# Expert gate and up, retention input and first modulation weights laid out by the host, 4 KB to a partition

## What is computed

```python
c_act = jax.nn.silu(c)
for i in range(2):
    mod = c_act @ ada_w + ada_b
    sh1, sc1, g1, sh2, sc2, g2 = jnp.split(mod, 6, axis=-1)
    h = modulate(rmsnorm(x, n1), sh1, sc1)
    m = retention_mixer(h, *mix_p, row, col) if i == 0 else gqa_mixer(h, *mix_p, row, col)
    x = x + g1[:, None, :] * m
    h = modulate(rmsnorm(x, n2), sh2, sc2)
    f = swiglu(h, *ffn_p) if i == 0 else moe_swiglu(h, *ffn_p)
    x = x + g2[:, None, :] * f
return modulate(rmsnorm(x, final_norm_g), fsh, fsc)

# retention: proj = h @ w_in            w_in (1024, 6144)
# moe: top 2 of 8 experts;  swiglu = (silu(h @ w_gate) * (h @ w_up)) @ w_down
#      w_gate, w_up (8, 1024, 3584), w_down (8, 3584, 1024)
```

## Time and profile before

| | us |
|---|---|
| Median of three runs | 1553.6 |
| The three runs | 1553.60, 1554.18, 1545.27 |
| The profiled execution, its own time | 1550.78 |
| Its span, first to last instruction | 1548.6 |
| TensorE busy | 1493.6 (96%) |
| VectorE busy | 1340.8 (87%) |
| ScalarE busy | 992.5 (64%) |
| GpSimd busy | 206.8 (13%) |
| Moved by DMA | 508.71 MB, mean 328 GB/s |

### The profile page before, as it was taken

The page is one execution under the profiler, slowest core; times in us unless marked ns, Lnnn a source line. Parts: engine busy times, 40 slices in busy tenths (PEclk is TensorE's granted clock), DMA queues, the critical chain, the costliest instruction groups (busy, mean ns, idle before and its releaser), DMA issues.

```text
span 1548.6 us, 20483 instructions
## 1 busy us (share of the span) xinstructions
PE 1493.6 (96%) x6796; PEld 1221.8 (79%) x6796; DVE 1340.8 (87%) x1083; ACT 992.5 (64%) x826; POOL 206.8 (13%) x188
## 2 busy tenths in 40 slices
PE   6999998999999999999999999999999999999996
PEld 6777676788877787778888888888888888887885
DVE  6899878888889689998998988988888988988898
ACT  4554344444447566677777777777777777777674
POOL 0499800000020011001001001001001001000320
PEclk9999999999999989999999999999999999999999
DMA  9989826899875379999999999999999999999993
GB/s 338 390 302 350 294 80 233 283 314 310 295 267 177 108 285 356 389 343 384 387 362 381 385 371 372 384 368 370 384 369 366 393 368 371 386 368 333 391 394 139
DMA packets 238897, 508.71 MB, mean 328 GB/s; under 512 B 15494, under 2 KB 38150, under 8 KB 238728
## 3 DMA queue, kind: packets, MB, share of 16 engines
q1 hardware_dynamic: 233824, 491.52, 87.2%
q0 software_dynamic: 4448, 14.55, 2.6%
q10 hardware_dynamic: 584, 2.11, 0.3%
HBM read 502.12 MB, written 7.87 MB: 329 GB/s over the span
## 4 chain that ended last, share of the span: by engine, by line
PE 72%; DVE 9%; POOL 7%; DMA 5%; ACT 3%; issue 3%; SPq 1%; ACTq 0%; DVEq 0%; POOLq 0%
PE bank L2051 22%; PE bank L2053 22%; PE bank L2052 22%; DVE lo L1794 3%; DMA stage<-in_l_moe_w_up 2%; PE bank L2475 1%; POOL proj L655 1%; POOL proj L654 1%; POOL ropet L651 1%; POOL ropet L650 1%; POOL ropet L652 1%; POOL proj L653 1%; DMA stage<-in_l_moe_w_gate 1%; PE bank L2157 1%; DMA stage<-in_l_ret_w_in 1%
## 5 line engine op out<-in xcount | busy, mean ns | idle before, releaser
L1794 DVE TENSOR_TENSOR lo<-stage,hi 128x2048 fp32r<-128x2048 f32 x168 | 388.4, 2319 | 41.9 <-ACT hi L1118 41.2
L1118 ACT CAST hi<-stage 128x2048 fp32r<-128x2048 f32 x168 | 321.9, 1918 | 106.0 <-DMA stage<-in_l_moe_w_up 91.1
L2052 PE MATMUL bank<-lo,hg_hi 128*128 128x512 f32 x892 | 348.2, 390 | 0.0
L772 ACT CAST hi<-stage 128x2048 fp32r<-128x2048 f32 x68 | 130.3, 1918 | 106.8 <-PE bank L2053 78.4
L2052 PEld LDWEIGHTS bank<-lo,hg_hi 128*128 128x128 f32 x892 | 168.1, 188 | 33.4
L1260 DVE TENSOR_TENSOR lo<-stage,hi 128x2048 fp32r<-128x2048 f32 x68 | 157.2, 2315 | 24.0 <-ACT hi L772 18.1
L1794 DVE TENSOR_TENSOR lo<-stage,hi_h 128x2048 fp32r<-128x2048 f32 x56 | 128.3, 2292 | 55.9 <-ACT hi_h L1118 55.9
L2051 PE MATMUL bank<-hi,hg_hi 128*128 128x512 f32 x448 | 174.5, 390 | 1.0 <-DVE lo L1794 1.0
L2052 PE MATMUL bank<-lo,eaT_hi 128*128 128x512 f32 x448 | 174.4, 389 | 0.0
L2053 PE MATMUL bank<-hi,hg_lo 128*128 128x512 f32 x448 | 174.3, 389 | 0.0
L2051 PE MATMUL bank<-hi,hT_hi 128*128 128x512 f32 x400 | 162.7, 407 | 2.3 <-DVE hT_lo L1323 2.1
(11 more groups left out here) (378 smaller groups left out, 2801.7 us busy)
## 6 DMA issues: line engine op xcount, KB each, us to landing
stage<-in_l_moe_w_gate SPq DMA_DIRECT2D x224, 512.0 KB, 5.1
stage<-in_l_moe_w_up SPq DMA_DIRECT2D x224, 512.0 KB, 5.6
stage<-in_l_moe_w_down SPq DMA_DIRECT2D x224, 512.0 KB, 5.4
ada_w<-in_l_ada_w SPq DMA_DIRECT2D x40, 1024.0 KB, 5.7
stage<-in_l_ret_w_in SPq DMA_DIRECT2D x48, 512.0 KB, 8.7
stage<-in_l_ffn_w_gate SPq DMA_DIRECT2D x22, 512.0 KB, 7.5
stage<-in_l_ffn_w_up SPq DMA_DIRECT2D x22, 512.0 KB, 8.7
stage<-in_l_ffn_w_down SPq DMA_DIRECT2D x22, 512.0 KB, 8.5
```

What stands on the lines that cost most here:

```text
L772: nc.scalar.copy(hi_of(b), stage[:, b % RING, :]).then_inc(hi_done, 1)
L1118: nc.scalar.copy(hi_e(b), stage[:, b % RING, :]).then_inc(hi_done, 1)
L1794: nc.vector.tensor_tensor(lo[:, b % RING, :], stage[:, b % RING, :], hi_e(b).bitcast(F32), ALU.subtract).then_inc(lo_done, 1)
L2052: mm(dst_ap, a_hi, w_lo, start=False, stop=False)
```

## The change

The host lays four tensors out anew before the launch, and the loads follow. A unit of `l0_ret_w_in`, `l1_moe_w_gate` and `l1_moe_w_up` becomes 128 rows of 2048 contiguous floats, one to a partition, so that each of its two DMAs is the first or second 4 KB of every 8 KB row (`load_laid`). A new input, `ada_pre`, holds the columns of shift and scale of the first modulation matrix, so that a piece of `pre_w` is one contiguous 4 KB a partition. The order of the loads, their sizes, their waits and semaphores, and what is in each buffer afterwards are as before. The other tensors keep their form. The host's work lies outside the time.

```diff
             l1_moe_w_router, l1_moe_b_router, l1_moe_w_gate, l1_moe_w_up, l1_moe_w_down,
-            final_ada_w, final_ada_b, final_norm_g, consts, dist, columns, out):
+            final_ada_w, final_ada_b, final_norm_g, consts, dist, columns, ada_pre, out):
     ctx = ExitStack()
...
-        w_in_v, w_out_v = rows(l0_ret_w_in), rows(l0_ret_w_out)
+        w_out_v = rows(l0_ret_w_out)
         fg_v, fu_v, fd_v = rows(l0_ffn_w_gate), rows(l0_ffn_w_up), rows(l0_ffn_w_down)
         qkv_v, ao_v = rows(l1_attn_w_qkv), rows(l1_attn_w_out)
-        mg_v = l1_moe_w_gate.rearrange("e (k p) n -> e p k n", p=P)
-        mu_v = l1_moe_w_up.rearrange("e (k p) n -> e p k n", p=P)
         md_v = l1_moe_w_down.rearrange("e (k p) n -> e p k n", p=P)
...
+            def load_laid(b, src, more=0):
+                sp.wait_ge(w_used, b + more + 1)
+                for part in (slice(0, UW // 2), slice(UW // 2, UW)):
+                    sp.dma_start(stage[:, b % RING, part], src[:, part]).then_inc(w_load[b % RING], 16)
             def load_ada(c, half, w, bias, col, more=0):
...
-                src = rows(l0_ada_w)[:, k, 0:2 * D].rearrange("p (s n) -> p s n", s=2)
-                sp.dma_start(pre_w[half][:, k], src[:, :, half * HALF:(half + 1) * HALF]).then_inc(pre_load[half * KT + k], 16)
+                src = ada_pre[half * KT + k].rearrange("p (s n) -> p s n", s=2)
+                sp.dma_start(pre_w[half][:, k], src).then_inc(pre_load[half * KT + k], 16)
...
                 cc, kg = in_unit(u)
-                load(U_RET + u, w_in_v[:, 4 * kg:4 * kg + 4, cc * CB:(cc + 1) * CB])
+                load_laid(U_RET + u, l0_ret_w_in[2 * cc + kg])
...
                 load_pre(0, k)
-            first = stage[:, 0, :].rearrange("p (k n) -> p k n", k=4)
-            sp.dma_start(first[:, 0:2, :], w_in_v[:, 0:2, 0:CB]).then_inc(w_first, 16)
+            sp.dma_start(stage[:, 0, 0:UW // 2], l0_ret_w_in[0, :, 0:UW // 2]).then_inc(w_first, 16)
             sp.sem_inc(w_load[0], 16)
-            sp.dma_start(first[:, 2:4, :], w_in_v[:, 2:4, 0:CB]).then_inc(w_load[0], 16)
+            sp.dma_start(stage[:, 0, UW // 2:UW], l0_ret_w_in[0, :, UW // 2:UW]).then_inc(w_load[0], 16)
             load_in(1)
...
                 load(U_AOUT + k, ao_v[:, 4 * kg:4 * kg + 4, n * CB:(n + 1) * CB])
-            def load_gate_up(e, b, col, more):
-                for m, wv in ((0, mg_v), (2, mu_v)):
+            def load_gate_up(e, b, j, more):
+                for m, wv in ((0, l1_moe_w_gate), (2, l1_moe_w_up)):
                     for g in range(2):
-                        load(b + m + g, wv[e, :, 4 * g:4 * g + 4, col] if isinstance(e, int) else
-                             wv[bass.ds(e, 1), :, 4 * g:4 * g + 4, col].rearrange("a p k n -> p (a k) n"), more)
+                        at_row = j * (2 * P) + g * P
+                        load_laid(b + m + g, wv[e, bass.ds(at_row, P), :] if isinstance(e, int) else
+                                  wv[bass.ds(e, 1), bass.ds(at_row, P), :].rearrange("a p n -> p (a n)"), more)
...
                     jm = j * 6 - 6
-                    load_gate_up(e, U_MOE + 4, bass.ds(j * ECH, ECH), more + jm)
+                    load_gate_up(e, U_MOE + 4, j, more + jm)
                     load_down(e, U_MOE + 8, j * 4 - 4, more + jm)
...
-            load_gate_up(0, U_MOE, slice(0, ECH), 0)
+            load_gate_up(0, U_MOE, 0, 0)
             for half in range(2):
...
                 before = sp.value_load(meta[0:1, bass.ds(w - 1, 1)], min_val=0, max_val=E - 1)
-                load_gate_up(e, U_MOE - 2, slice(0, ECH), w * UNITS_ITEM)
+                load_gate_up(e, U_MOE - 2, 0, w * UNITS_ITEM)
                 load_down(before, U_MOE + 2, 4 * (N_EC - 1), w * UNITS_ITEM)
...
     given["columns"] = np.ascontiguousarray(np.concatenate([v.reshape(-1, P).T for v in first], axis=1))
+    pre = given["l0_ada_w"][:, 0:2 * D].reshape(KT, P, 2, 2, HALF)
+    given["ada_pre"] = np.ascontiguousarray(pre.transpose(3, 0, 1, 2, 4)).reshape(2 * KT, P, 2 * HALF)
+    w_in = given["l0_ret_w_in"].reshape(2, 4, P, N_IN, CB)
+    given["l0_ret_w_in"] = np.ascontiguousarray(w_in.transpose(3, 0, 2, 1, 4)).reshape(2 * N_IN, P, UW)
+    for name in ("l1_moe_w_gate", "l1_moe_w_up"):
+        w = given[name].reshape(E, 2, 4, P, N_EC, ECH)
+        given[name] = np.ascontiguousarray(w.transpose(0, 4, 1, 3, 2, 5)).reshape(E, N_EC * 2 * P, UW)
     arrays, args = {}, []
...
```

## The result

| | before | after |
|---|---|---|
| Median, 20 runs each | 1549.9 us | 1554.4 us |
| Lowest and highest | 1543.4, 1554.2 | 1551.8, 1561.1 |
| Ratio after to before, 95% interval | | 1.0039 (1.0027 to 1.0051) |
| Profiled execution, its time | 1550.8 | 1556.6 |
| Its span | 1548.6 | 1554.5 |

The kernel is slower by 0.4%: the two medians differ by 4.5 us, the ratio stands for 6 us. The forecast was 5 to 6 us less, 1547.5 us. The time lies in the stated range and within 1% of before, but it moved the other way. That it lies in the range is no merit of the sum: its upper end, 1556, was set from no gain at the highest of the three runs known then (median 1553.6), and the median of twenty runs before is 1549.9.

The account below looks back on a forecast made before the run. TensorE was taken to set the pace in the middle items, with transfers hidden. Terms 0.5 + 2.0 + 0.5 + 1.0 + 1.0 = 5.0 us, and 1.1 more, off 1553.6 gave 1547.5 us, range 1539 to 1556.

Parts of the forecast that it names:

- What bounds the kernel: Middle items of expert work: TensorE sets the pace at 2.84 us a unit, SP waits for buffers, transfers are hidden.
- The transfer term: Gate and up units: 4 KB packets save 0.12 us a unit, 2.71 to 2.59, bounds 0 and twice that.
- Issue: SP's issue of a gate DMA falls from 383 ns to near 345 ns, which gains nothing.
- The start: 0 to 60 us: earlier first piece 0.1 and no wait before `lo` 0.4, together 0.5 us less.
- The first item: 565 to 670 us: VectorE bounds; faster transfer in four chunks gives 2.0 us less, bounds 0 and 3.3.
- The items in the middle: Short cast delays at the seams between items: 0.5 us less, bounds 0 and 0.7.
- The rival with the other sign: New layout slower to read, deciding above 2.97 us a unit; 1570 us at 3.05; chance of over 1% slower 0.06.
- The last item: 1386 to 1505 us: 1.0 us less from the long wait, bounds 0 and 4.0, and 1.0 from the `lo` waits.
- A sign of the forecast: Whole kernel: packets fewer by a third to a half at the same bytes.
- The 1.1 us that I took off the median: Whole kernel: besides the sum, 1.1 us less because faster transfers may shorten late transfers in the slower runs.

Follow-up runs that it names:

- e4_2kb_packets: The changed kernel's layout, but gate and up loaded in packets of 2 KB, 2 KB of every 4 KB; ratio to the kernel before 1.0191.
- e7_pitch_10kb: The changed kernel with 2 KB of padding behind each 8 KB row of gate and up; ratio to the kernel before 0.9963.
- e5_rows_early: The changed kernel with the split of the next item's rows moved ahead of the second gate unit's cast and split; ratio to the kernel before 1.0000.
- e2_experts_only: The kernel before with only gate and up in the new form, start loads as before; ratio to the kernel before 1.0069.
- e3: The changed kernel, but each half of a gate or up unit is one piece of 512 KB in HBM; ratio to the kernel before 0.9976.
- e1_start_only: The kernel before with only retention input and first modulation in the new form, gate and up as before; ratio to the kernel before 0.9996.
- e11_pitch_18kb: The changed kernel with gate and up rows side by side plus 2 KB padding, 4 KB of every 18 KB; ratio to the kernel before 0.9981.

## Why the prediction was wrong

*What bounds the kernel.* Right: middle items run at TensorE's pace, SP waits for buffers. The six items between the first and the last seam are full, but for one late landing at most, with every layout whose median landing is 5 us or less.

*The transfer term.* Right in sign and near in size where the DMA engines are saturated. Casts that waited in the first item, start us first:

```profile
603.38 1.92 ACT L1122 CAST hi<-stage 128x2048 fp32r<-128x2048 f32 x1 [0.17 <-DMA stage<-in_l_moe_w_down]
605.92 1.92 ACT L1122 CAST hi_m<-stage 128x2048 fp32r<-128x2048 f32 x1 [0.63 <-DMA stage<-in_l_moe_w_down]
...
608.76 1.91 ACT L1122 CAST hi_h<-stage 128x2048 fp32r<-128x2048 f32 x1 [0.43 <-DMA stage<-in_l_moe_w_gate]
611.31 1.92 ACT L1122 CAST hi_r<-stage 128x2048 fp32r<-128x2048 f32 x1 [0.64 <-DMA stage<-in_l_moe_w_gate]
```

Gate units now come 608.76 to 611.31, 2.55 us apart instead of 2.71, down 2.54. The saving, 0.16 us, is above my 0.12 and inside its bound of twice that. Two of the experiments say what it hangs on. Two gate units of e4_2kb_packets, 2 KB of every 4 KB, and two of e7_pitch_10kb, 4 KB of every 10 KB, in the same stretch:

```profile
603.07 1.91 ACT L1127 CAST hi_h<-stage 128x2048 fp32r<-128x2048 f32 x1 [0.31 <-DMA stage<-in_l_moe_w_gate]
605.78 1.92 ACT L1127 CAST hi_r<-stage 128x2048 fp32r<-128x2048 f32 x1 [0.80 <-DMA stage<-in_l_moe_w_gate]
```

```profile
603.03 1.91 ACT L1122 CAST hi_h<-stage 128x2048 fp32r<-128x2048 f32 x1 [0.15 <-DMA stage<-in_l_moe_w_gate]
605.59 1.92 ACT L1122 CAST hi_r<-stage 128x2048 fp32r<-128x2048 f32 x1 [0.65 <-DMA stage<-in_l_moe_w_gate]
```

They are 2.71 and 2.56 us apart. So in a full queue packets of 2 KB take 2.71 us a unit at pitches of 4 and 14 KB, packets of 4 KB take 2.55 us at 8 and 10 KB: the rate follows the packet, not the pitch. The Trainium skill's fixed cost of a packet ("DMA: Bandwidth & Descriptors", "Why small descriptors are slow (HBM only)"), by which I had estimated 0.06 us, gives too little here.

*Issue.* Right. SP's gate issue went from 383 to 333 ns in the median and changed nothing:

```profile
L503 SPq DMA_DIRECT2D stage<-in_l_moe_w_gate x224: 327/333/1070, 489.5 to 1505.1; - x112
```

*The start.* The steps were right. The wait of 0.42 us before `lo` is gone, and VectorE's steps keep their 1.3 us:

```profile
9.37 0.75 DVE L1350 TENSOR_SCALAR hs<-pre_w,cact 128x1024 f32<-128x1024 f32 x1 [9.25 <-DMA pre_w<-in_ada_pre]
...
12.67 9.19 DVE L1352 SCALAR_TENSOR_TENSOR hs<-pre_w,cact,hs 128x1024 f32<-128x1024 f32 x7
...
32.72 2.29 DVE L1264 TENSOR_TENSOR lo<-stage,hi 128x2048 fp32r<-128x2048 f32 x1
34.93 7.88 DVE L1352 SCALAR_TENSOR_TENSOR hs<-pre_w,cact,hs 128x1024 f32<-128x1024 f32 x6
```

The last six start at 34.93 instead of 36.24, 1.3 us earlier, where I had 0.5: the first piece landed 0.9 us earlier (9.37 instead of 10.24), not 0.1. But it came back at once. TensorE, which had stood idle for these steps, starts its next work earlier and is on the lower of its two clock levels: the mean granted clock of the stretch 45 to 60 is 0.75 after. It was 0.80 before:

```profile
45.00:60.00 15.00, 15.00 (x61) 12.74 (x61) 10.30 (x15) 8.03 (x8) 1.09 (x2) 0.80 1.04 393
```

Rotation on GpSimd starts at 60.86 after and 60.84 before. The experiment with the start alone (0.9996) agrees that the net is nothing I can measure. I had put the term down as kept because the work behind it was full; I had not asked at which clock that work starts. When the lower clock falls differs from one execution to the next, so these two settle no more than themselves: with the same start layout, the execution of e5_rows_early has 1.00 in this stretch and its rotation starts at 56.71, and with the old start e2_experts_only has 0.89 and 58.67.

*The first item.* Direction right, size too large. The waits for `eact` fell from 4.0 to 2.1 us, which looks like the 2.0 us of the term, but only one of them fell for the change. These end the second of the four chunks, before and after:

```profile
631.45 0.66 PE L2475 MATMUL bank<-cst,eact 128*128 128x128 f32 x4 [1.44 <-DVE eact L1849]
```

```profile
633.20 0.66 PE L2479 MATMUL bank<-cst,eact 128*128 128x128 f32 x4 [0.73 <-DVE eact L1853]
```

This chunk took 18.53 us and takes 17.82, 0.7 us less. The next two took 18.67 and 18.65 us and take 18.65 and 18.63: in them ScalarE reaches a gate cast late because it waits for TensorE in front of it (2.92 us for a sum of modulation, L2026), not for a transfer. With the layouts of e2, e3, e4 and e7 these two chunks take 18.63 to 18.67 us as well, so they do not depend on the transfer. The wait of 0.89 us at 578.08 is gone, but there TensorE was at the lower clock for longer (0.97 in the stretch 565 to 670, 0.99 before) and came about 3 us later itself. e5_rows_early, with the same layouts, has 1.00 in that stretch and that wait (0.79 us), so the 3 us belong to this execution and are no part of the explanation. The term, put at 2.0 us, is worth about 0.7.

*The items in the middle: the step that failed.* I wrote that with a transfer of 2.59 us for 2.84 us of TensorE's work "in the new form these units would only wait longer for TensorE". That set a rate against a rate. The seam hangs on a latency, from SP's issue to the landing of the first gate unit, and I took it as a thing that could only shorten with the packets. It rose from 5.1 to 6.45 us at the seam shown, against a slack of about 0.2 us (VectorE done at 806.56, TensorE needs it at 806.75). Seven waits of 0.9 to 1.3 us, 7.6 us in all, outweigh the gains; from the first to the last seam the kernel takes 6.6 us more, where I had put 0.5 us less. I had bounded this term by 0 and a gain of 0.7 us, without a loss. That is the error in the sum. A row that shows how little slack there is was at hand: the wait of 2.33 us stands at a seam. I called it a chance event, which it is, but it also says that a landing a few us late is not absorbed there.

*The rival with the other sign* named the mechanism, 4 KB of every 8 KB in a regular pattern, but priced it as a rate. By that price nothing is lost until a unit takes 2.97 us, and units took 2.55. The loss begins well below that price, since latency is lost first. The evidence that I set against it, attention output weights with 2 KB of every 4 KB landing in 4.5 us, was read where the DMA engines are not full (share 0.68 from 468.7 to 487.0 us, where these units are loaded). In the experts' stage the same pattern (e4_2kb_packets) costs 1.9%. The Trainium skill's entry on row pitches of large powers of two ("DMA: Bandwidth & Descriptors", "Latency and other measured facts") starts at 512 KiB; the runs show a loss from pitches of 4, 8 and 16 KB, and its remedy, padding, works here with 2 KB. It tells the loss as a rate, while here the rate in a full queue is kept and the landing is late.

*The last item.* From its seam on it takes 2.3 us less, near the 2.0 us of my two terms, but not for their reasons, so this is luck. The long wait of 2.33 us is not repeated, and one of 1.02 us takes its place. It is absent with the old layout of gate and up too (e1_start_only, 0.2 us of seam waits in all), so it belonged to that one execution. The waits for `lo` grew from 1.0 to 1.6 us instead of vanishing.

*A sign of the forecast.* "Packets fewer by a third to a half" does not follow from its own count: 65,536 of 238,897 packets are 27%, and 27% went. The 1.1 us that I took off the median besides the sum, for late transfers in the slower runs, is shown by no run.

**What stays open.** No run here shows where in HBM a packet goes, so that a part of the places serves a pattern with holes is inferred from pitch and padding, not shown. Whether it is powers of two or multiples of 4 KB that are late is not tested. Nor is it settled why 2 KB of every 4 KB costs more than 4 KB of every 16 KB, and why the landing suffers while the rate in a full queue does not.

## What to carry to other kernels

When the host lays weights out, give each DMA either a range in one piece or a padded row pitch (here 10 and 18 KB were good, 4, 8 and 16 KB were not), and check the median landing in the stage that is busy, not only the packet size. A prefetch that keeps up in rate can still be late at a seam, where an engine in a fixed order waits for the newest landing before it does what the critical engine needs next; put that work ahead of the landing, or measure the slack there. A term bounded by "no loss" needs a row that excludes the loss.

## What the runs showed of the hardware

With nothing changed but a padding of 2 KB, gate's 4 KB packets at a pitch of 8 KB land in 5.6 us in the median and at a pitch of 10 KB in 4.7 us, up's in 6.3 and 5.0 us; with gate and up side by side it is 5.9 us at 16 KB and 4.9 us at 18 KB. In one piece gate's land in 4.5 us. In the saturated stretch of the first item the pattern shows no loss: 2.55 us a unit at 8 KB and 2.56 us at 10 KB, and 405 GB/s by the row below, where packets of 2 KB had 393. So the loss is in the landing of single transfers, in the items where TensorE sets the pace.

After waits of 1.3 us or less at the seams TensorE's granted clock stayed at 1.00; after waits of 2.4 and 2.7 us (e2_experts_only) matmuls ran 0.43 us apart instead of 0.23 for some 3 us, which, with the longer wait itself, makes such an item 3 us longer than one with a short wait. After one of 2.42 us (e11_pitch_18kb) this did not happen.

The row of the saturated stretch:

```profile
615.40:633.20 17.80, 17.07 (x76) 13.74 (x77) 17.49 (x13) 11.50 (x9) 0.00 (x0) 1.00 1.03 405
```
